# Ordering the matmuls of a wide unit: all long ones first, or long and short ones in turn

## The reference, cut to what matters

```python
h = jnp.einsum('bsd,de->bse', x, w_in[i])            # 2048 x 8192: v, q and k, pool, gates
...
q = jnp.einsum('bsd,de->bse', x, wq).reshape(B, S, PEER_HEADS, 2, PEER_HALF)
...
ug = jnp.take(u_tab, ib, axis=0)
h = jnp.einsum('td,tkd->tk', xb, ug)
a = (jax.nn.gelu(h.astype(jnp.float32), approximate=False) * gb).astype(xb.dtype)
return jnp.einsum('tk,tkd->td', a, vg)
```

## Time and profile before

| | |
|---|---|
| median of 3 runs | 2343.66 us (2342.65 to 2346.1) |
| the profiled execution | 2347.04 us, of it 2345.4 us span |
| TensorE matmul busy | 2270.3 us, 97% of the span |
| TensorE weight load busy | 2003.3 us, 85% |
| VectorE busy | 1560.8 us, 67% |
| ScalarE busy | 1040.5 us, 44% |
| mean granted TensorE clock | 0.989 |

### The profile page before, as it was taken

How to read it: one execution, slowest core, us unless ns; L and a number is a source line. 1 busy time by engine, 2 the same in 40 slices (tenths; PEclk the granted TensorE clock), 3 DMA queues, 4 the chain that set the end, 5 groups by cost and what they waited for, 6 DMA issues and landing times.

```text
span 2345.4 us, 41611 instructions
## 1 busy us (share of the span) xinstructions
PE 2270.3 (97%) x13200; PEld 2003.3 (85%) x13200; DVE 1560.8 (67%) x2870; ACT 1040.5 (44%) x1430; POOL 44.0 (2%) x89
## 2 busy tenths in 40 slices
PE   6999999899899999999999999999999999999996
PEld 5887888898688888888899999998888888888885
DVE  6547566655744479998888888888555555555556
ACT  4444555544444354445543333333444444444442
POOL 1000000000000000001000000000000000000000
PEclk9999999999999999999999999999999999999998
DMA  7555555455555556565554444554666666666663
GB/s 248 182 185 164 180 180 176 153 182 179 170 174 166 194 173 200 185 205 191 188 171 156 156 158 156 161 160 150 192 194 196 203 199 202 201 206 203 202 195 118
DMA packets 115715, 425.32 MB, mean 181 GB/s; under 512 B 13352, under 2 KB 13368, under 8 KB 114528
## 3 DMA queue, kind: packets, MB, share of 16 engines
q1 hardware_dynamic: 112608, 412.14, 55.0%
q0 software_dynamic: 3072, 12.72, 1.7%
HBM read 420.60 MB, written 6.31 MB: 182 GB/s over the span
## 4 chain that ended last, share of the span: by engine, by line
PE 85%; DVE 8%; issue 3%; DMA 2%; ACT 1%; DVEq 0%; SPq 0%; ACTq 0%
PE ps L1348 25%; PE ps L1328 17%; PE ps L1355 12%; PE ps L1334 9%; PE ps L1316 6%; PE ps L1312 6%; PE ps L1311 6%; DVE w_lo L760 2%; PE ps L1586 2%; DMA raw<-in_u 1%; DMA ln_gb<-in_ln_in 1%; DMA raw<-in_w_in 0%; DVE bn L773 0%; DVE experts L1192 0%; DVE x L779 0%
## 5 line engine op out<-in xcount | busy, mean ns | idle before, releaser
L453 ACT ACTIVATE w_hi<-raw 128x1024 fp32r<-128x1024 f32 x774 | 821.4, 1061 | 1045.6 <-DMA raw<-in_peer_v 366.9
L760 DVE TENSOR_TENSOR w_lo<-raw,w_hi 128x1024 fp32r<-128x1024 f32 x774 | 946.0, 1223 | 489.6 <-PE ps L1355 429.7
L1328 PE MATMUL ps<-x_t_hi_lo,w_hi 128*128 128x512 f32 x2304 | 582.5, 395 | 4.5 <-ACT ple_gate L658 2.4
L1348 PE MATMUL ps<-w_hi,x_t_hi_lo 128*128 128x512 f32 x2304 | 571.2, 390 | 3.2 <-DVE x_t_hi_lo L1247 2.5
L1348 PEld LDWEIGHTS ps<-w_hi,x_t_hi_lo 128*128 128x128 f32 x2304 | 433.7, 188 | 93.6 <-issue 3.5
L1328 PEld LDWEIGHTS ps<-x_t_hi_lo,w_hi 128*128 128x128 f32 x2304 | 415.0, 189 | 82.7 <-issue 7.2
L1334 PEld LDWEIGHTS ps<-x_t_hi_lo,w_lo 128*128 128x128 f32 x2304 | 314.9, 191 | 29.2 <-DVE w_lo L760 7.2
L1334 PE MATMUL ps<-x_t_hi_lo,w_lo 128*128 128x256 f32 x2304 | 323.7, 284 | 3.3 <-DVE w_lo L760 3.0
L1355 PE MATMUL ps<-w_lo,x_t_hi_lo 128*128 128x512 f32 x1152 | 309.2, 390 | 0.0
L1311 PE MATMUL ps<-x_t_hi_lo,w_hi 128*128 128x256 f32 x1024 | 260.5, 292 | 1.2 <-DVE experts L843 1.2
L1355 PEld LDWEIGHTS ps<-w_lo,x_t_hi_lo 128*128 128x128 f32 x1152 | 217.3, 189 | 45.3
(11 more groups left out here) (213 smaller groups left out, 1344.9 us busy)
## 6 DMA issues: line engine op xcount, KB each, us to landing
raw<-in_u SPq DMA_DIRECT2D x256, 512.0 KB, 4.1
raw<-in_peer_v SPq DMA_DIRECT2D x256, 512.0 KB, 4.8
raw<-in_w_in SPq DMA_DIRECT2D x128, 512.0 KB, 4.1
raw<-in_branch SPq DMA_DIRECT2D x32, 512.0 KB, 4.0
raw<-in_wout SPq DMA_DIRECT2D x32, 512.0 KB, 3.7
raw<-in_wq SPq DMA_DIRECT2D x32, 512.0 KB, 3.8
raw<-in_pleg SPq DMA_DIRECT2D x32, 512.0 KB, 4.1
x<-in_x SPq DMA_DIRECT2D x2, 1024.0 KB, 6.3
```

The costliest lines, as they stand in the source:

```text
L453: nc.scalar.activation(HI[:, u % 4, :], RAW[:, u % 4, :], ACT.Copy).then_inc(hi_ready, 1)
L760: v.tensor_tensor(LO[:, u % 2, :], RAW[:, u % 4, :], HI[:, u % 4, :].bitcast(F32), ALU.subtract) \
L1328: mm(PS[:, bank, :], w(HI, u % 4)[:, k, :], XHL[:, 8 * half + k, :, :].rearrange("p a t -> p (a t)"), start=(half == 0 and k == 0), stop=F ...
L1348: mm(nbank(tt, 2 * half + q), stn[:, tt * P:(tt + 1) * P], HI[:, u % 4, q * 512:(q + 1) * 512], start=(first and s == 0), stop=False, skip ...
```

## The change

Within each wide unit the sixteen matmuls are put in another order. The same sixteen are issued, with the same operands. Before: L L L L L L L L S S S S S S S S. After: L L L L L S L S L S L S S S S S. The wait for the low part stands before the first short matmul, as before, which is now the sixth matmul and not the ninth. The wait for the high part, and the count of `unit_done` on the last short matmul, stay. Narrow units are not touched, nor is anything on another engine.

```diff
-                def his():
-                    for k in range(8):
-                        mm(PS[:, bank, :], w(HI, u % 4)[:, k, :],
-                           XHL[:, 8 * half + k, :, :].rearrange("p a t -> p (a t)"),
-                           start=(half == 0 and k == 0), stop=False)
-
-                def los():
-                    for k in range(8):
-                        r = mm(PS[:, bank, 0:S], w(LO, u % 2)[:, k, :], XH[:, 8 * half + k, :], start=False,
-                               stop=(half == 1 and k == 7))
-                    return r
-
-                use(i, per, u, his, los)
+                def high(k):
+                    mm(PS[:, bank, :], w(HI, u % 4)[:, k, :],
+                       XHL[:, 8 * half + k, :, :].rearrange("p a t -> p (a t)"),
+                       start=(half == 0 and k == 0), stop=False)
+
+                def low(k):
+                    return mm(PS[:, bank, 0:S], w(LO, u % 2)[:, k, :], XH[:, 8 * half + k, :], start=False,
+                              stop=(half == 1 and k == 7))
+
+                pe.wait_ge(hi_ready, val(i, per, u + 1))
+                for k in range(5):
+                    high(k)
+                pe.wait_ge(lo_ready, val(i, per, u + 1))
+                for k in range(8):
+                    r = low(k)
+                    if k < 3:
+                        high(5 + k)
+                r.then_inc(unit_done, 1)
```

## The result

The changed kernel takes 2349.94 us (median of 13 runs, 2345.76 to 2352.81) against 2343.81 us before (13 runs); the ratio is 1.0023, 95% interval 1.0015 to 1.0031, so +5.4 us (3.5 to 7.3). A second timing beside another set of runs gave 1.0022 (1.0011 to 1.0032). It is slower, just past the 0.2% that can be told from no change.

A forecast was written before the change was run, and what follows sets the result against it. TensorE's matmul order was taken to bound the kernel everywhere save where VectorE leads. The order's -0.9 us and the earlier wait's +4.3 us summed to +3.4 us, 2347.0 us on the median, range 2337 to 2356.

The forecast's parts named there:

- Loads hardly bound the shorts, so there is little to hide: Wide units: a short at 120 ns is above the 110 ns floor set by loads, so hiding loads gains little.
- The three longs that now follow a single short cost 233 and not 227 ... Net -3 ns a unit.: Wide units: shorts save 21 ns, longs cost 18 more; times 288 units, -0.9 us (bounds -47 to +34 ns a unit).
- The prediction's own sign of being wrong: Undisturbed wide units differing by over 15 ns from 2.795 us, or a short's load starting before the long ahead of it.
- The gate loop, 1.57 us: Gate loop: the third unit's low part comes 0.22 us late for the earlier wait, in all 7 passes, 1.57 us.
- The u stage, 0.68 us: u stage: VectorE keeps the pace where it leads; only the last stall leaves TensorE 0.68 us later, carried to the end.
- VectorE waits for the end of unit 59 at the join ... so the 0.65 goes on to the low part of 61.: Pool stage: unit 58's 0.65 us stall passes through VectorE's wait for TensorE at the join to unit 61's low part.
- the 2.01 us: Pool stage and start of gate: low part of unit 65 comes 1.33 later, plus three longs behind its wait, 2.01 us.
- Part 2: The wait for the low part comes three longs sooner: 2.01 + 1.57 + 0.68 = 4.26 us, from nothing to 7.0.
- Each change back to a long starts its slow run anew: Rival, wide units: +34 ns a unit, +9.8 us, with waits +14.1 us, 2357.8; slower, chance 0.22.
- The order costs nothing and the waits more: Rival: 0 for the order and 7.0 us for the waits, 2350.7; slower, chance 0.13.
- Nothing moves: Rival: the stalls are absorbed and the transitions between long and short cancel, 2343.7; chance 0.08.
- Shorts hidden under longs: Rival, wide units: longs' excess vanishes, each short after a long costs 113 ns; -13.5 + 4.3 = -9.2 us, 2334.4; chance 0.17.

The follow-up runs named there:

- the wait alone: The kernel before with its order kept and only the wait for the low part moved ahead of the sixth long: 2346.33 us, ratio 1.0008 (1.0000 to 1.0017).

## Why the prediction was right in its number and wrong in its parts

Point by point:

- *The number.* 2347.0 against 2349.9, within 2337 to 2356; "within 0.2%, on the slow side" came out as slower by 0.23%. Two terms were off, one by +4.4 us and one by -2.3, and partly cancelled. That they cancelled, and brought the sum within 3 us, was luck.
- *Loads hardly bound the shorts, so there is little to hide.* Right: no short went below 112 ns in any order, and each order with more changes was dearer at the common pace. The difference of 107 ns between a settled long and a settled short said so beforehand.
- *"The three longs that now follow a single short cost 233 and not 227 ... Net -3 ns a unit."* This term was mis-sized: +20 ns a unit, within the bounds of -47 and +34. The shorts save 9 ns where 21 were reckoned; the longs cost 29 and not 18, since the second and third take 241 and 236. I had applied the first distance of the run-in to all three, though the row beside it, 236 for the second long of a run, warned that the run-in doesn't fall steadily. Also 20 ns are not to be multiplied by 288: VectorE's region, wq and half of the gate units pay nothing or little. Instead of -0.9 us it was +3.5. The prediction's own sign of being wrong, units over 15 ns from 2.795, was met: 2.813 is 18 ns off.
- *The gate loop, 1.57 us.* Right: 1.6 alone, 1.34 with the mixed order.
- *The u stage, 0.68 us.* Right in mechanism. 0.8 alone; in the changed kernel 0.44 net, since the earlier growth of units is swallowed where VectorE leads. VectorE doesn't wait for TensorE before a low part there, as foretold. The prediction misread one row on the way: in the earlier trace rows VectorE's slices show 9 tenths from 880 to 1055 us only, and 8 tenths from there to 1640. Nothing in the sum hung on it.
- *"VectorE waits for the end of unit 59 at the join ... so the 0.65 goes on to the low part of 61."* The stall of 0.65 itself came (0.65 with the wait alone). But the step from it to VectorE failed, and the same step at unit 63. The join waits for ScalarE's copy, and that stood behind a rounding that waited for a load. So the 2.01 us were 0.9 in the kernel with the wait alone and 0.2 in the changed one. In the changed one a part of the difference is the clock's: its slow stretch at 221 us fell more into the pause (unit 65 takes 1.17 us more, unit 66 0.66 less). The growth at this place, 0.4, 0.2, 0.6 and 1.9 us in the four profiles of the changed kernel, moves with these stretches, so the clock's share can't be separated. For the same reason the start of the gate stage came 0.8 us later and not 1.3, the end of its second unit 1.1 and not 2.0.
- *Part 2 in all:* 4.3 foretold. By the starts 2.0 in the changed kernel and 3.4 (0.89 + 1.63 + 0.84) in the kernel with the wait alone, whose time says 1.9 (0 to 4).
- *The rivals.* "Each change back to a long starts its slow run anew" is nearest: it decides from +1.5 ns a unit and the change has +20, but not at its full price of +34. "The order costs nothing and the waits more" has a time, 2350.7, nearer to the measured one than the forecast's, but both its parts fell: the order costs 3.5 us and not 0, the waits 2.0 and not 7.0. "Nothing moves" fell with the gate loop. "Shorts hidden under longs" fell, except for stretches at the quicker pace, which show that about its half size is possible.

What stays open is what makes the run-in of the longs, and what chooses between the two paces. The rows exclude the weights' tile as the cause, and a stall as the only one. The pool stage, where quicker stretches appear in three orders, is written out and not a hardware loop, but the u stage, a loop, has one as well.

## What to carry to other kernels

Before mixing long and short matmuls to hide weight loads, subtract the settled distances: if a short costs a long less just its columns, loads don't bind it, and in this kernel each further change of length cost 5 to 14 ns. A wait moved forward costs only in the units where its margin was thin, and those can be listed from starts and ends in the trace. When such a delay is to be carried on by another engine, look at what stands ahead in that engine's queue: the releaser that a row names may itself have been held by something else.

## What the runs showed of the hardware that I had not expected

- One order of matmuls has two steady paces in one execution: 2.813 and 2.787 us for sixteen matmuls, each within a nanosecond or two over up to 61 units in a row; 2.826 (mean of 2.830, 2.830 and 2.819) and 2.774 when fully in turn. The order of before showed only 2.793.
- A change of length costs for several matmuls: after shorts the longs take 233, 236, 228, 233, 231 ns before they settle at 227.
- The number of stretches at the lower clock level varied from one execution to the next: six, five, seven and seven in four profiles of the changed kernel, nine in that of before. The three by which the two profiles compared differ moved the span by 4.5 us.
